# A two-layer decoder trunk on one core: the first weight block in halves, warming products at the head, roots in two GpSimd steps, and a weight split moved ahead of the exponents

## What is computed

```python
for i in range(2):
    xn = rmsnorm(h, pre_g[i])
    y = conv_gmlp_mixer(xn, ...) if i == 0 else mlstm_mixer(xn, ...)
    h = h + rmsnorm(y, post_g[i])
    gate = sigmoid(rmsnorm(h, ple_g[i]) @ w_ple_gate[i])
    h = h + gate * (p[i] @ w_ple[i])

# rmsnorm(x, g) = x * rsqrt(mean(x * x) + 1e-6) * g, over the 1024 columns
# inside the mLSTM, per head and chunk, with the forget and input gates in d:
p_mat = exp(d - m_t) * (q @ k.T)
num = inter_scale * (q @ c_prev) + p_mat @ v
den = inter_scale * (q @ n_prev) + sum(p_mat)
hc = num / max(abs(den), exp(-m_t)), then a root mean square norm per head
```

## Time and profile before

| What | Value |
|---|---|
| median of 3 runs | 1013.74 us |
| the profiled execution | 1012.66 us |
| its span, first to last instruction | 1010.8 us |
| TensorE busy | 980.2 us (97%) |
| VectorE busy | 641.6 us (63%) |
| ScalarE busy | 506.0 us (50%) |
| GpSimd busy | 91.7 us (9%) |
| mean granted TensorE clock | 0.997 of full speed |

### The profile page before, as it was taken

How to read it: one execution, slowest core, us unless ns; L and a number is a source line. 1 busy time by engine, 2 the same in 40 slices (tenths; PEclk the granted TensorE clock), 3 DMA queues, 4 the chain that set the end, 5 groups by cost and what they waited for, 6 DMA issues and landing times.

```text
span 1010.8 us, 12035 instructions
## 1 busy us (share of the span) xinstructions
PE 980.2 (97%) x4486; PEld 801.3 (79%) x4486; DVE 641.6 (63%) x863; ACT 506.0 (50%) x832; POOL 91.7 (9%) x148
## 2 busy tenths in 40 slices
PE   6999999999999999998999999999999999999998
PEld 4888888888877888786777878878887888888776
DVE  5757788787874235558986765665567577421835
ACT  6454545555552234536556556456654675341722
POOL 2020110100000003103000001010101000000500
PEclk9999999999999999999999999999999999999999
DMA  9555946847351522422937465573838164242122
GB/s 359 182 147 145 275 141 167 218 163 202 73 199 41 215 84 105 167 84 95 266 114 192 125 167 142 150 172 120 212 126 205 40 167 146 84 167 84 46 80 83
DMA packets 24760, 150.37 MB, mean 149 GB/s; under 512 B 3072, under 2 KB 4224, under 8 KB 8448
## 3 DMA queue, kind: packets, MB, share of 16 engines
q1 hardware_dynamic: 18800, 106.63, 27.7%
q0 software_dynamic: 5904, 42.99, 21.8%
HBM read 145.42 MB, written 4.19 MB: 148 GB/s over the span
## 4 chain that ended last, share of the span: by engine, by line
PE 84%; DVE 7%; ACT 4%; issue 2%; POOL 2%; DMA 1%; POOLq 0%; DVEq 0%; ACTq 0%
PE bank L2034 16%; PE bank L2037 16%; PE bank L2036 15%; PE bank L1961 8%; PE bank L1963 8%; PE bank L1962 8%; DVE w_lo L1309 3%; PE bank L2287 1%; PE bank L2058 1%; ACT square L683 1%; PE bank L2060 1%; PE bank L2059 1%; PE bank L2291 1%; ACT w_hi L719 1%; PE bank L2269 1%
## 5 line engine op out<-in xcount | busy, mean ns | idle before, releaser
L1309 DVE TENSOR_TENSOR w_lo<-raw,w_hi 128x1024 fp32r<-128x1024 f32 x204 | 240.8, 1222 | 156.3 <-ACT w_hi L719 155.9
L2034 PE MATMUL bank<-w_hi,l_hi 128*128 128x512 f32 x784 | 322.4, 411 | 9.5 <-DVE bank L1405 3.8
L2037 PE MATMUL bank<-w_hi,l_lo 128*128 128x512 f32 x784 | 307.3, 392 | 0.0
L2036 PE MATMUL bank<-w_lo,l_hi 128*128 128x512 f32 x784 | 306.5, 391 | 0.0
L719 ACT ACTIVATE w_hi<-raw 128x1024 fp32r<-128x1024 f32 x204 | 204.6, 1055 | 60.1 <-DMA raw<-in_slots 43.3
L2034 PEld LDWEIGHTS bank<-w_hi,l_hi 128*128 128x128 f32 x784 | 147.6, 188 | 44.8 <-issue 9.9
L2037 PEld LDWEIGHTS bank<-w_hi,l_lo 128*128 128x128 f32 x784 | 147.6, 188 | 31.9
L2036 PEld LDWEIGHTS bank<-w_lo,l_hi 128*128 128x128 f32 x784 | 147.9, 189 | 30.0 <-issue 1.0
L1274 DVE TENSOR_TENSOR w_lo<-raw,w_hi 128x1024 fp32r<-128x1024 f32 x52 | 61.3, 1221 | 116.8 <-ACT w_hi L672 116.7
L672 ACT ACTIVATE w_hi<-raw 128x1024 fp32r<-128x1024 f32 x52 | 52.3, 1057 | 132.1 <-PE bank L1963 122.5
L1961 PE MATMUL bank<-w_hi,y_hi 128*128 128x512 f32 x224 | 90.7, 405 | 0.2 <-DVE y_lo_end L1487 0.2
(11 more groups left out here) (221 smaller groups left out, 1194.1 us busy)
## 6 DMA issues: line engine op xcount, KB each, us to landing
raw<-in_slots SPq DMA_DIRECT2D x86, 1024.0 KB, 6.4
raw<-in_slots POOLq DMA_DIRECT2D x41, 1024.0 KB, 8.8
h<-in_x SPq DMA_DIRECT2D x8, 512.0 KB, 5.9
out<-h SPq DMA_DIRECT2D x4, 512.0 KB, 4.3
h<-out SPq DMA_DIRECT2D x4, 512.0 KB, 6.8
out<-h SPq DMA_DIRECT2D x8, 256.0 KB, 2.0
p_sb<-in_p SPq DMA_DIRECT2D x2, 512.0 KB, 3.8
g_post<-in_g_rows SPq DMA_DIRECT2D x2, 512.0 KB, 5.6
```

The lines of the kernel that those rows point to most:

```text
L1309: dve.tensor_tensor(w7_lo[:, ring(g), c], raw7[:, source(*STEPS[g]), c], w7_hi[:, ring(g), c].bitcast(F32), ALU.subtract).then_inc(w7_lo_r ...
L2034: pe.matmul(dst[:, :], left_hi, w7_hi[:, r, c], start=(first and k == 0), stop=False, skip_group_check=True)
L2036: pe.matmul(dst[:, :], left_hi, w7_lo[:, r, c], start=False, stop=False, skip_group_check=True)
L2037: done = pe.matmul(dst[:, :], left_lo, w7_hi[:, r, c], start=False, stop=(k == 3), skip_group_check=True)
```

## The change

Five things change.

1. The first weight block is loaded in two halves with a semaphore each (`w_first`), and split by `first_high` and `first_low` half by half; on ScalarE and VectorE the halves are interleaved with the splits of the first transposed tokens (`first_left`, `left`), and the squares of token tile 2 move behind `first_left(1)`. Waits on `x_raw_in` count one less.
2. TensorE does twelve 128-column products of the identity with itself at its very start, in place of the two 512-column products after the first transposes.
3. `rstd_of` has two GpSimd steps: the squares carry a scale of 1/sqrt(D), and one `tensor_scalar` adds both half sums and eps, with the second half sum as a per-partition operand.
4. In `odd_qv`, step k = 2, `hi7` of step 4 goes ahead of `exponents` and the two `s5_copy`.
5. Every square gets the scale of point 3 (`square_any`), which changes no number of instructions.

```diff
@@ sync
-        block_in(0, B11, BX, x_raw_in)
+        for half in range(2):
+            c = slice(half * SLOT // 2, (half + 1) * SLOT // 2)
+            sp.dma_start(raw7[:, BX, c], slots[B11][:, c]).then_inc(w_first[half], 16)
@@ gpsimd, rstd_of
-            link(pool.tensor_tensor(dst, first, second, ALU.add))
-            link(pool.tensor_scalar(dst, dst, 1.0 / D, EPS, ALU.mult, ALU.add))
+            link(pool.tensor_scalar(dst, first, second, EPS, ALU.add, ALU.add))
             pool.tensor_tensor(dst, dst, minus_half[:, 0:1], ALU.pow).then_inc(done, 1)
@@ scalar
-            act.activation(square[:, 0:SEQ], src, ACT.Square, accum_out=dst).then_inc(done, 1)
+            act.activation(square[:, 0:SEQ], src, ACT.Square, scale=float(D) ** -0.5, accum_out=dst).then_inc(done, 1)
...
+        def first_high(half):
+            c = slice(half * SLOT // 2, (half + 1) * SLOT // 2)
+            act.wait_ge(w_first[half], 16)
+            act.activation(w7_hi[:, ring(0), c], raw7[:, BX, c], ACT.Copy).then_inc(w7_hi_ready, 1)
...
-        hi7(0)
-        first_left(0)
-        x_squares(2)
-        first_left(1)
+        first_high(0)
+        first_left(0, (0,))
+        first_high(1)
+        first_left(0, (1,))
+        first_left(1)
+        x_squares(2)
         first_full(0)
@@ scalar, odd_qv
                 if k == 2:
+                    hi7(step_of(u, k) + 2)
                     exponents(x + 1)
                     for tp in range(2):
                         s5_copy(u, tp)
+                    continue
@@ vector
-        lo7(0)
+        first_low(0)
         left(0, 0, 0, 1)
+        first_low(1)
+        left(0, 1, 0, 1)
         left(0, 0, 1, 2)
         first_norm(2)
-        left(0, 1, 0, 1)
         left(0, 1, 1, 2)
@@ tensor
         pe.wait_ge(ident_ready, 1)
+        for n in range(12):
+            done = pe.matmul(b_of(0)[:, 0:P], ident[:, :], ident[:, :], start=True, stop=True)
+        done.then_inc(warm, 1)
         first_transpose(0, 0)
-        for tp in range(2):
-            done = pe.matmul(b_of(tp)[:, :], ident[:, :], h[:, 0, 0:SEQ], start=True, stop=True)
-        done.then_inc(warm, 1)
         first_transpose(0, 1)
```

More of the change, by code:

```diff
@@ L364, in trunk @@
     a_in = sem("a_raw_in")
+    w_first = [sem("w_first0"), sem("w_first1")]
     w7_hi_ready = sem("w7_hi_ready")
@@ L699, in hi7 @@
             u, p = STEPS[g]
-            if p in (1, 11):
-                act.wait_ge(x_raw_in, 16 * (u + 1))
+            if p == 1:
+                act.wait_ge(x_raw_in, 16 * u)
             if p in (2, 21):
@@ L746, in left_sum, with first_left @@
             act.activation(l_hi[:, L_PLACE[p]], src[:, :, :], ACT.Copy).then_inc(lhs_hi[p], 1)
-        def first_left(t):
+        def first_left(t, parts=range(2)):
             at = slice((t % 2) * P, (t % 2 + 1) * P)
-            for q, p in enumerate((1, 2) if t < 2 else (21, 4)):
+            for q in parts:
+                p = ((1, 2) if t < 2 else (21, 4))[q]
                 act.wait_ge(first_xt, 2 * t + q + 1)
@@ L1328, in s5_add @@
         def s5_add(u):
-            dve.wait_ge(x_raw_in, 16 * (u + 1))
+            dve.wait_ge(x_raw_in, 16 * u)
             dve.wait_ge(v_raw_in, 16 * phase(u) + 16)
@@ L1385, in _, with first_low @@
         dve.wait_ge(g_in, 16)
+        def first_low(half):
+            c = slice(half * SLOT // 2, (half + 1) * SLOT // 2)
+            dve.wait_ge(w7_hi_ready, half + 1)
+            dve.tensor_tensor(w7_lo[:, ring(0), c], raw7[:, BX, c], w7_hi[:, ring(0), c].bitcast(F32),
+                              ALU.subtract).then_inc(w7_lo_ready, 1)
         first_norm(0)
         first_norm(1)
-        lo7(0)
+        first_low(0)
         left(0, 0, 0, 1)
+        first_low(1)
+        left(0, 1, 0, 1)
         left(0, 0, 1, 2)
         first_norm(2)
-        left(0, 1, 0, 1)
         left(0, 1, 1, 2)
```

## The result

The changed kernel takes 1007.5 us, the median of 4 runs (1007.37 to 1008.66), beside 1014.31 us (1013.7 to 1016.38) for the kernel before. The ratio is 0.9936, with a 95% interval of 0.9918 to 0.9954: 6.5 us faster, between 4.7 and 8.3. The forecast was 1008.2 within 1004.9 to 1011.9. The profiled execution took 1007.52 us with a span of 1005.7, 5.1 less than the span before.

What follows compares the result with a forecast made beforehand. TensorE is busy 97% of the span, so only its idle time can be won. 0.0 + 2 x 0.84 + 0.6 + 3.2 = 5.5 us, giving 1007.2 profiled, 1008.2 forecast; 8 in 10 between 1004.9 and 1011.9.

Steps and rivals of the forecast that it cites:

- The head: Start to second weight block: products start 1.6 us earlier but at the low clock, 0.0 won, bounds +0.7 and -1.2.
- the step that put that block at 21.5: Head: squares of tile 3 and the root each 0.3 us earlier, so the second weight block comes at about 21.5.
- The roots: Tails and seam: one of three GpSimd steps goes, 0.84 us won per tail and 0.6 at the seam.
- the one for tile 2: Tails: the step held from 397.75 to 398.98 is gone, so `gated` of tile 2 starts 0.9 us earlier.
- The split: Units 9, 11, 13: `hi7` runs in ScalarE's idle time, ending TensorE's waits behind `c_make`; 3.2 us, bounds 4.2 and 0.5.
- the 1.0 for SyncE's earlier load: Units 9, 11, 13: the earlier load delays the landing; 0.2, 0 and 0.8 us come back as waits.
- The clock: Tail's wait, shrinking from 1.84 to about 1.5 us: whether the clock falls behind it left open; one fall costs 1.7.
- the third rival: End of first tail: the clock no longer falls, since the idle time is shorter; 1.7 us more, 1006.5, chance 0.12.
- the last rival: Slower: the clock falls at more places, four named, 1.7 us each, head another 1.0; 1016, chance 0.04.
- The first: Units 9, 11, 13: the early load takes the split's gain, leaving it 0.5 us; 1010.9, chance 0.15.
- second: Head: the clock holds and the second weight block at 21.5 decides; 0.7 us more, 1007.5, chance 0.12.
- fourth rivals: Roots: a per-partition operand makes one step as long as two, tails and seam give nothing; 1010.5, chance 0.07.

Runs made afterwards that it cites:

- the kernel with norm 3 first: The changed kernel with VectorE's norm of tile 3 and the first low part after it ahead of a weight split in both tails: 1004.02 us, ratio 0.9917.
- the held-back load: The changed kernel with SyncE's load of the 21 block in units 9, 11 and 13 held until both c_make are done: 1006.39 us, ratio 0.9944.

## Why the prediction came out as it did

The time was right to 0.7 us and the places were right, but three of its four terms were off, and they made up for one another, which is luck. The sentence that TensorE never waits elsewhere was wrong too: at the seam it also waits 1.28, 2.48 and 1.88 us (at 472.77, 486.74 and 512.44 in the kernel before). The change leaves these as they are, so the sum did not suffer.

**The head, 0.0 forecast.** Right in sum (+0.15 in the profile, 1.0001 alone) and in what it said of the clock: it was down again when the products began. The transposes of tile 1 took 1.97 us, the first four products are 0.42 to 0.59 us apart, and the row for this stretch has the granted clock at 0.50:

```profile
14.00:16.00 2.00, 2.00 (x7) 1.51 (x6) 2.00 (x4) 1.71 (x5) 0.00 (x0) 0.50 1.01 426
```

TensorE came to the second block at 21.74, and not at 22.1, and waited 0.57 us. Wrong was the step that put that block at 21.5: VectorE's chain brings it at 22.31. The one step with a per-partition operand takes 0.30 us, not 0.19. The squares of tile 2 moved behind the splits and start at 14.87 instead of 13.30, and so those of tile 3 start at 17.20 instead of 16.87, where the forecast had them 0.3 us earlier. In the kernels with this head the block comes at 22.0 to 22.4 and once at 22.70. So the head never won more than 0.15 us, and the 0.0 came out because VectorE's chain ended where TensorE's work was forecast to.

**The roots, 2 x 0.84 + 0.6 = 2.3 forecast, 1.3 measured** (0.56 and 0.49 in the tails, 0.2 at the seam). The mechanism held for the first wait of each tail. The step that failed is the one for tile 2: the held step at 397.75 was taken as gone, and `gated` of tile 2 and all behind it as 0.84 to 0.9 us earlier. In the kernel with the roots alone the power step comes in its place and is itself held (1.49 us from 397.12), so `gated` of tile 2 starts 0.56 earlier, counted from `yb`. VectorE's weight split moves by the same 0.57, not by 0.8: ScalarE's copies ahead of it wait for TensorE's products, and TensorE gained no more than its one wait. Behind the split the two held steps follow as forecast. A step that is held costs what is left of the instruction that holds it, so taking out a step ahead of it gives little here; the kernel with norm 3 first shows the 1.88 us go to 0.57. At the seam the second root was taken for 0.3 and gave nothing, with the same cause likely (VectorE's gate beside it), which I did not test.

**The split, 4.2 - 1.0 = 3.2 forecast, 4.0 to 4.5 measured.** The 1.40 per unit were right, or slightly low. The term that was mis-sized is the 1.0 for SyncE's earlier load. The load comes 2.3 us earlier, as worked out, but in the changed kernel no wait comes back. How much of the landing is the load's stays open: the held-back load allows 0 to 0.5 us per unit. And the landing moves by more than that for a reason I don't have. In the four kernels that have the change's split but not its early products it is late enough that waits before the piece h = 8 do come back, 0.2 to 0.5 us each in units 9 and 13, 0.5 to 0.9 in sum; in the changed kernel's second profile it is 0.19 in unit 13. So the nothing that came back in the changed kernel is in part luck. That the piece is just in time, in unit 13, was right:

```profile
777.73 0.48 DVE L1725 SCALAR_TENSOR_TENSOR state<-state,sc,bank 128x257 f32<-128x257 f32 x1
...
778.26 0.70 PE L2308 MATMUL bank<-v_odd,expo 128*128 128x257 f32 x2
```

The state ends at 778.21 and the piece starts at 778.26, with no idle time to speak of.

**The clock.** "Whether the clock still falls behind it I can't say" was the right answer. With idle times of 1.84 to 1.88 us it fell in the first tail in four kernels of this study (the kernel before, the split alone, no warming, the split after the exponentials) and not in five others. A fall costs 1.5 to 1.6 us in the tails and 1.2 to 1.45 at the seam; 1.7 was forecast. In the changed kernel's profile the third rival's event came true, the clock did not fall in the first tail, though its reason did not, since the idle time was as long as before. It fell behind the second tail's instead, one of the four places that the last rival named. The two cancel in this profile, which is luck. The first, second and fourth rivals' cases did not come true.

**What I had not seen.** The split that starts earlier holds GpSimd's other root, the one per head (lines 649 and 650 after): its two steps take 1.61 and 1.92 us in unit 9, where they took 0.83 and 1.04. No wait of TensorE follows from it there, so it costs nothing.

## What to carry to other kernels

Read how long the idle engine's wait lies ahead of a blocked in-order instruction: an independent one that can run inside that wait is nearly free to move ahead, and here it brought most of the gain. Shortening a chain pays only up to the next thing that ends there; when a step in the chain is held by another engine's instruction, move that instruction, not the step. Look at where warm-up work ends: here the early products ended 7 us ahead of the first real one, and the clock was down again by then. And it is worth only what the next chain leaves.

## What the runs showed of the hardware

A GpSimd step of one element per partition takes 0.19 us with constant operands, 0.30 with a per-partition one, and 0.56 as a power; beside a VectorE instruction with both inputs in SBUF it took up to 1.6 us and ended 0.1 to 0.4 us after that. The Trainium skill (SBUF — State Buffer, Who interferes with whom) says that a VectorE instruction with two SBUF inputs contends with a GpSimd instruction that reads SBUF, that the ports they share are locked for one of them, and that the order of issue decides who waits. The trace agrees with the first half. For the order the step at 407.45 in the kernel with the roots alone says nothing, although it began 0.2 us ahead of the weight split, since VectorE was then still in the norm of tile 2 (406.46 to 407.73), which also has two inputs in SBUF. This place in unit 9 of the changed kernel says more:

```profile
580.21 1.61 POOL L649 TENSOR_TENSOR msq<-msq,eps_tile 128x4 f32<-128x4 f32 x1
580.23 0.42 DVE L1722 COPY state<-bank 128x257 f32<-128x257 f32 x1
580.56 2.35 DVE L1322 TENSOR_TENSOR w_lo<-raw,w_hi 128x1024 fp32r<-128x1024 f32 x2
```

The GpSimd step began 0.35 us ahead of the weight split, beside a copy from PSUM, and was held all the same, to just behind the split's first half, while the split's two halves took their usual 2.35 us. So the starts that the trace shows don't tell who goes first.

The same idle time of TensorE before the same transposes brought its clock down in some kernels and not in others that differ elsewhere, and two profiles of the changed kernel itself differ in where it fell (behind 954.86 in one, behind 484.61 in the other). Each fall costs 1.2 to 1.6 us. In a comparison of single profiles of kernels that differ by 2 us, that is nearly as much as the change.
